# A rotary embedding whose inputs are freed by ScalarE and whose sums are made in SBUF, and two reorderings around it, in a two-block float32 kernel

## The reference, cut to what matters

```
proj = u @ in_w                                  # c_q (384), c_kv (256), k_r (64), z (2048)
q = (rms_norm(c_q, q_norm_w) @ uq_w)             # 16 heads of 128 + 64
kv = (rms_norm(c_kv, kv_norm_w) @ ukv_w)         # 16 heads of 128 (k) + 128 (v)
q_nope, q_rope = q[..., :128], rope(q[..., 128:], positions)
k_rope = rope(k_r, positions)                    # one for all heads
s = ([q_nope, q_rope] . [k_nope, k_rope]) * 192 ** -0.5, causal softmax, times v
o = o.reshape(...) * silu(z);  y = o @ out_w

rope(x): [x1 * cos - x2 * sin, x2 * cos + x1 * sin]
```

## Time and profile before

| | us |
|---|---|
| median of three runs | 941.56 |
| lowest, highest | 941.27, 942.48 |
| the profiled execution | 941.56 |
| its span in the trace | 939.7 |
| PE busy | 882.5 |
| mean granted TensorE clock | 0.973 of full |

### The profile page before, as it was taken

How to read it: one execution, slowest core, us unless ns; L and a number is a source line. 1 busy time by engine, 2 the same in 40 slices (tenths; PEclk the granted TensorE clock), 3 DMA queues, 4 the chain that set the end, 5 groups by cost and what they waited for, 6 DMA issues and landing times.

```text
span 939.7 us, 18247 instructions
## 1 busy us (share of the span) xinstructions
PE 882.5 (94%) x7019; PEld 847.8 (90%) x7019; DVE 555.1 (59%) x1569; ACT 481.9 (51%) x920; POOL 620.6 (66%) x274
## 2 busy tenths in 40 slices
PE   7999899999999899999999896978999999999995
PEld 7999899989998899999999885867899999999995
DVE  5987567762244434443369867676556666651165
ACT  6745555544445465555545265444464445554451
POOL 3899645547886355557777895333387888888980
PEclk9999999998999999999999898989999999999997
DMA  8666533333665234444645575131364666656631
GB/s 321 182 218 208 155 109 91 90 91 103 188 181 161 87 112 117 133 133 140 193 141 166 156 211 158 50 91 45 90 180 158 194 188 190 183 179 179 202 90 46
DMA packets 38534, 138.85 MB, mean 148 GB/s; under 512 B 4272, under 2 KB 4272, under 8 KB 38448
## 3 DMA queue, kind: packets, MB, share of 16 engines
q1 hardware_dynamic: 38448, 137.69, 48.7%
HBM read 136.63 MB, written 1.05 MB: 147 GB/s over the span
## 4 chain that ended last, share of the span: by engine, by line
PE 72%; DVE 11%; ACT 3%; issue 1%; POOL 1%; DVEq 0%; ACTq 0%
PE ps L541 19%; PE ps L542 19%; PE ps L543 19%; DVE ps L1526 2%; PE ps L566 1%; PE ps L737 1%; PE ps L739 1%; POOL wl L502 1%; PE ps L652 1%; PE ps L548 1%; PE ps L574 1%; DVE nnm L1680 1%; ACT wh L974 1%; PE ps L549 1%; PE ps L550 1%
## 5 line engine op out<-in xcount | busy, mean ns | idle before, releaser
L502 POOL TENSOR_TENSOR wl<-raw,wh 128x1024 fp32r<-128x1024 f32 x254 | 609.2, 2420 | 277.8 <-ACT wh L974 277.7
L541 PE MATMUL ps<-uh,wh 128*128 128x256 f32 x1248 | 354.8, 284 | 7.0 <-DVE ul L1461 3.0
L542 PE MATMUL ps<-ul,wh 128*128 128x256 f32 x1248 | 350.3, 281 | 0.0
L543 PE MATMUL ps<-uh,wl 128*128 128x256 f32 x1248 | 350.0, 280 | 0.0
L974 ACT ACTIVATE wh<-raw 128x1024 fp32r<-128x1024 f32 x256 | 263.0, 1054 | 121.5 <-PE ps L543 118.3
L541 PEld LDWEIGHTS ps<-uh,wh 128*128 128x128 f32 x1248 | 236.1, 189 | 12.1 <-issue 3.6
L542 PEld LDWEIGHTS ps<-ul,wh 128*128 128x128 f32 x1248 | 236.1, 189 | 0.0
L543 PEld LDWEIGHTS ps<-uh,wl 128*128 128x128 f32 x1248 | 235.6, 189 | 0.0
L1619 DVE TENSOR_TENSOR h<-ps,h 128x256 f32<-128x256 f32 x32 | 13.6, 424 | 118.0 <-PE ps L543 117.8
L542 PE MATMUL ps<-ffl,wh 128*128 128x256 f32 x176 | 49.3, 280 | 0.0
L541 PE MATMUL ps<-ffh,wh 128*128 128x256 f32 x176 | 49.1, 279 | 0.0
(11 more groups left out here) (361 smaller groups left out, 1794.8 us busy)
## 6 DMA issues: line engine op xcount, KB each, us to landing
raw<-slabs SPq DMA_DIRECT2D x256, 512.0 KB, 3.8
h<-x_fm SPq DMA_DIRECT2D x4, 256.0 KB, 5.4
out_fm<-outb SPq DMA_DIRECT2D x4, 256.0 KB, 2.2
cst<-shape_consts SPq DMA_DIRECT2D x1, 768.0 KB, 7.9
vec<-vectors SPq DMA_DIRECT2D x1, 303.5 KB, 4.0
pin<-p_fm SPq DMA_DIRECT2D x1, 256.0 KB, 5.7
```

The source lines that it names most:

```text
L502: nc.gpsimd.tensor_tensor(wl[:, s % PART_RING, :], raw[:, s % RAW_RING, :], wh[:, s % PART_RING, :].bitcast(f32), ALU.subtract).then_inc(s ...
L541: nc.tensor.matmul(res, w_h, a_h, start=first, stop=False)
L542: nc.tensor.matmul(res, w_h, a_l, start=False, stop=False)
L543: ins = nc.tensor.matmul(res, w_l, a_h, start=False, stop=last)
```

## The change

Five things are altered.

1. The `qr` projections have "act" as their consumer in the table: their bank is free when ACT has copied it to `rx`, no longer when DVE has read it. DVE's product with cos reads `rx` in SBUF.
2. The product with sin goes from `PS_TR` to a new SBUF tile `r1`, and signals `rope_swapped_read`. The add reads `r1` and `r2` in SBUF.
3. `rope_swap` waits for `rope_swapped_read` (the product) and not for `rope_out` (the add).
4. On ACT, `high_parts(n_q)` stands ahead of the copies of `v0`, no longer behind them. `feed("v0")`, which splits the slabs up to five ahead of `v0`'s, stands ahead of both, as it did.
5. On PE, `scores(0)` stands between the projections of head 0 and those of head 1.

```diff
-        add(f"qr{i}", "mla_uq_w", cols, "dve")
+        add(f"qr{i}", "mla_uq_w", cols, "act")
...
             def rope_swap(i):
 
-                if i:
-                    pe.wait_ge(sem("rope_copied"), i)
-                else:
-                    pe.wait_ge(sem("dve_evac"), freed[jobs["kr"].out][1])
+                who, count = freed[jobs[rope_job(i)].out]
+                pe.wait_ge(sem(f"{who}_evac"), count)
+                wait(pe, "rope_swapped_read", i)
+                if i == 0:
                     wait(pe, "xdt", 16)
-                wait(pe, "rope_out", i)
                 nc.tensor.matmul(PS_TR[:, 0:T], swap, rx[:, i % 2, :], start=True, stop=True)\
...
             head_proj(0)
+            scores(0)
             head_proj(1)
-            scores(0)
             scores(1)
...
             high_parts(n_kv)
+            feed("v0")
+            high_parts(n_q)
             for n in range(4):
                 for t in range(TB):
                     o = output(f"v{n}", t)
                     nc.scalar.activation(vn[:, t, n * 512:(n + 1) * 512], o[:, :], ACT.Copy).then_inc(sem("act_evac"), 1)
-                if n == 0:
-                    high_parts(n_q)
             for i in range(8):
                 o = output(f"qr{i}")
                 wait(act, "rope_out", i)
-                nc.scalar.activation(rx[:, (i + 1) % 2, :], o[:, 0:T], ACT.Copy).then_inc(sem("rope_copied"), 1)
+                nc.scalar.activation(rx[:, (i + 1) % 2, :], o[:, 0:T], ACT.Copy).then_inc(sem("act_evac"), 1)
...
+                who, count = freed[jobs[rope_job(i)].out]
+                dve.wait_ge(sem(f"{who}_evac"), count)
+                wait(dve, "rope_out", i)
+                tt(r2[:], rx[:, i % 2, :], cos, ALU.mult).then_inc(sem("rope_cos"), 1)
+                dve.wait_ge(sem("rope_swap"), i + 1)
+                tt(r1[:], PS_TR[:, 0:T], sin, ALU.mult).then_inc(sem("rope_swapped_read"), 1)
+                dve.wait_ge(sem("rope_swapped_read"), i + 1)
+                dve.wait_ge(sem("rope_cos"), i + 1)
                 if i == 0:
-                    taken("kr")
-                    tt(r2[:], rx[:, 0, :], cos, ALU.mult).then_inc(sem("rope_cos"), 1)
+                    tt(kr[0:64, 0, :], r1[0:64, :], r2[0:64, :], ALU.add)
+                    tt(kr[64:128, 1, :], r1[64:128, :], r2[64:128, :], ALU.add).then_inc(sem("rope_out"), 1)
                 else:
-                    o = output(f"qr{i - 1}")
-                    dve.wait_ge(sem("rope_copied"), i)
-                    wait(dve, "rope_out", i)
-                    tt(r2[:], o[:, 0:T], cos, ALU.mult).then_inc(sem("dve_evac"), 1)
-                turned = PS_TR[:, 0:T]
-                dve.wait_ge(sem("rope_swap"), i + 1)
-                tt(turned, turned, sin, ALU.mult).then_inc(sem("rope_sin"), 1)
...
-                    tt(qr[:, i - 1, :], turned, r2[:], ALU.add).then_inc(sem("rope_out"), 1)
+                    tt(qr[:, i - 1, :], r1[:], r2[:], ALU.add).then_inc(sem("rope_out"), 1)
```

More of the change, by code:

```diff
@@ L313, in build @@
         cqr, ckr = ar("cqr", [3, T]), ar("ckr", [2, T])
-        rx, r2 = ar("rx", [2, T]), ar("r2", [T])
+        rx, r1, r2 = ar("rx", [2, T]), ar("r1", [T]), ar("r2", [T])
         cursor[0] = mark
@@ L467, in gain, with rope_job @@
             return v(name, at + k)
+        def rope_job(i):
+            return f"qr{i - 1}" if i else "kr"
         block = ctx.enter_context(nc.Block())
@@ L748, in prob_transpose @@
                 if hd == 0:
-                    wait(pe, "rope_out", 9)
+                    wait(pe, "rope_swapped_read", 9)
                 for c in range(3):
@@ L1641, in rotate @@
                     nc.vector.memset(kr[0:64, 1, :], 0.0)
+                who, count = freed[jobs[rope_job(i)].out]
[6 more added lines that the diff above has]
+                dve.wait_ge(sem("rope_cos"), i + 1)
                 if i == 0:
-                    taken("kr")
-                    tt(r2[:], rx[:, 0, :], cos, ALU.mult).then_inc(sem("rope_cos"), 1)
-                else:
-                    o = output(f"qr{i - 1}")
-                    dve.wait_ge(sem("rope_copied"), i)
-                    wait(dve, "rope_out", i)
-                    tt(r2[:], o[:, 0:T], cos, ALU.mult).then_inc(sem("dve_evac"), 1)
-                turned = PS_TR[:, 0:T]
-                dve.wait_ge(sem("rope_swap"), i + 1)
-                tt(turned, turned, sin, ALU.mult).then_inc(sem("rope_sin"), 1)
[L1653 to L1659, removed]
-                    tt(qr[:, i - 1, :], turned, r2[:], ALU.add).then_inc(sem("rope_out"), 1)
+                    tt(kr[0:64, 0, :], r1[0:64, :], r2[0:64, :], ALU.add)
+                    tt(kr[64:128, 1, :], r1[64:128, :], r2[64:128, :], ALU.add).then_inc(sem("rope_out"), 1)
+                else:
+                    tt(qr[:, i - 1, :], r1[:], r2[:], ALU.add).then_inc(sem("rope_out"), 1)
             for n in range(2):
```

## The result

The changed kernel takes 949.07 us (median of four runs, 948.33 to 949.59), the kernel before 942.02 on the same chip; the ratio is 1.0067, with a 95% interval of 1.0044 to 1.0092. It was forecast at 943.4, between 941.3 and 944.5. The direction that the sum had was right and the size was not: it is slower by some 6 to 7 us, not by 1.9. The profiled execution took 947.84.

What follows compares the result with a forecast made beforehand. PE was taken to bound the kernel. From 941.56 us, +2.13 (high parts), -1.2 - 0.46 (rotations) and -0.1 (scores) made +0.37, and a clock fall +1.5, giving 943.4, range 941.3 to 944.5.

Steps and rivals of the forecast that it cites:

- the sum: All terms added to 941.56: +0.37 us without the clock and +1.5 for the clock, giving 943.4.
- What bounds the kernel, and that a loss before the head loop stays: PE bounds the kernel; a microsecond it gains or loses before the head loop is gained or lost at the end.
- Edit 4: `v1` at 289.39, net 2.13: Passage v0 to v1: v1 waits for v0's first copy, begins 2.57 later, 0.44 is regained, qr0 2.13 later.
- The clock: a fall, +1.5: PE's new 2.33 us pause before v1 brings 1.2 GHz for 3.3 to 3.4 us, costing 1.5; chance 0.55.
- the rival without a fall: Clock stays up behind the pause before v1; time 941.9, no difference; chance 0.27.
- the long spell: Low clock behind the pause before v1 holds 6.6 us, as at 212.40; time 945.0; chance 0.07.
- the spared fall: Clock stays up behind the 2.16 pause before 618.30, returning 1.6 us; 940.3 with no fall before v1; chance 0.06.
- Edits 1 to 3: -1.2 - 0.46: Rotations: with the add out of the swap loop, six steps save 1.2 us and the last pair 0.46.
- The rival "the rotations are not faster": ACT's copy with a slab split, or DVE, replaces the add as bound; 943.6 without fall, 945.1 with; chance 0.05.
- Edit 5: -0.1: scores(0) ahead of head_proj(1): pause moves from before the transposes to before the scores, 0.1 saved, bounds -0.2 and +0.3.

Runs made afterwards that it cites:

- e7: e2 plus six idle matmuls on PE behind the spread, filling some 2 us of the pause; 945.58 against 944.57 for the kernel before, ratio 1.0013.
- e2: Kernel before with only the high parts of q moved ahead of the copies of v0; 946.43 against 943.26, ratio 1.0028.
- e5: Whole change, but with r1 and a copy of cos in PSUM; 944.67 against 944.57 for the kernel before, ratio 1.0003.
- e6: Whole change, with POOL's instruction cut to 64 of 1024 columns for seven slabs (time probe only); 945.57 against 944.57 for the kernel before, ratio 1.0011.
- e4: Kernel before with only the rotation changes, r1 and a copy of cos in PSUM; 940.62 against 943.26, ratio 0.9983.
- e3: Kernel before with only scores(0) moved ahead of head_proj(1); 943.74 against 943.26, ratio 0.9997.
- e8: e4 with the last swap moved behind the projections of head 0; 940.91 against 944.57 for the kernel before, ratio 0.9975.
- e1: Kernel before with only the rotation changes, high parts and scores order undone; 945.23 against 943.26, ratio 1.0023.
- e9: e1 with r1 alone in PSUM, the cos product still reading SBUF twice; one run of 942.81 beside 943.70 for the kernel before.

## Why the prediction was wrong, step by step

- *What bounds the kernel, and that a loss before the head loop stays.* Right: S to T grew by 6.03 and the span by 6.3.
- *Edit 4: `v1` at 289.39, net 2.13.* Right to 0.03: it began at 289.42, and e7, where the clock stays up, has 2.13. The profile names no releaser for this pause ("issue"). That it waits for the first copy of `v0` rests on that copy's start at 288.74, 0.68 ahead of `v1` where 0.67 was forecast, and on e2, where edit 4 alone brings the pause.
- *The clock: a fall, +1.5.* Right in kind; e2 less e7 gives 1.26. In e5, where the clock was already low when `v1` began, the same stretch less e7's is 1.51, so the price varies with where the low spell lies. The fall came in all four profiled executions with the pause unfilled (the changed kernel, e2, e5, e6), so the rival without a fall did not occur. Neither did the long spell (the changed kernel's lasted from 290.35 to 293.76) nor the spared fall (the clock fell again behind the pause that ends at 624.59). The argument was weaker than it looked, though. It took two lone pauses just over 2 us as a sign of what such a pause does, and other profiles have pauses of 2 to 3 us without a fall (last section). In the kernel before a pause of 1.82, ending at 213.18, coincides with a fall too, so 2.16 was not the shortest, as the rival of the spared fall has it.
- *Edits 1 to 3: -1.2 - 0.46.* **This is the step that failed.** The mechanism was there: with the hold removed (e4, e5, e6) the rotations take 1.97 less, even 0.3 more than forecast, and the last pair of swaps is 1.21 apart, where I had 1.28. What failed is the sentence "DVE's product with cos and its add now read SBUF only. I take them at the add's 0.42 at most". That duration had been taken from an add with one input in PSUM, and the only rotation product with two SBUF inputs in the trace, 0.35 us, was a single case. In the changed kernel the instructions stood for POOL's, and the stretch was 16.67 and not 12.98: 3.69 of the miss. The same passage says that no one waits for these instructions until `scores(0)`. That is wrong too. ACT's next copy into `rx` waits for the add (`rope_out`), and the sine product, which frees `PS_TR` for the next swap, stands behind the cos product on DVE. One such copy of the changed kernel:

```profile
309.47 0.38 ACT L1138 ACTIVATE rx<-ps 128x256 f32<-128x256 f32 x1 [2.65 <-DVE qr L1657]
```

- *The rival "the rotations are not faster"* had the copies on ACT as its mechanism and a chance of 0.05. ACT's copies were late as well, but as a consequence: they wait for `rope_out`, DVE's add. e4 has the same copies and is fast. Its price, no gain at all, was also too small, since a hold can cost more than the add had.
- *Edit 5: -0.1.* 0.0 by itself (e3), and +0.61 in the changed kernel, since it put `scores(0)` directly behind the last rotation: the cover of 1.77 of `head_proj(1)`, which I had costed at nothing for this wait, was gone when the add ended 1.7 late.

The forecast sum was 1.87. The measured parts are 2.13 + 1.26 + 2.03 + 0.61 = 6.03; the other 0.3 of the span's 6.3 lies outside these stretches.

What could have been read beforehand stands in two places. The first is the trace of the kernel before, far from the rotations. It has the same instruction, an add of 128x256 with two SBUF inputs, eight times at line 1994 (durations in ns: shortest, median, longest), and others besides:

```profile
L1994 DVE TENSOR_TENSOR h<-h,pt x8: 424/859/2228, 904.0 to 927.7; 128x256 f32<-128x256 f32 x8
```
```profile
494.45 2.44 DVE L1762 TENSOR_TENSOR cpad<-cvt,csg 128x256 f32<-128x256 f32 x1
570.28 2.29 DVE L1857 TENSOR_TENSOR nrr<-nrr,gates 128x2 f32<-128x2 f32 x1
913.48 2.23 DVE L1994 TENSOR_TENSOR h<-h,pt 128x256 f32<-128x256 f32 x1
```

POOL's instructions around the last three run from 494.22 to 496.61, 570.16 to 572.56 and 913.01 to 915.42, and each of DVE's ends just behind. A median of twice the shortest duration is the sign to look for.

The second place: the Trainium skill, "SBUF — State Buffer", section "SBUF: two separate sides", says that DVE and GpSimd share one pair of SBUF ports, exclusively and for a whole instruction, and that a DVE instruction takes part in it when it has two SBUF inputs and GpSimd's reads SBUF. The trace agrees (DVE's ends 0.28 or 0.29 behind POOL's, five times). POOL is busy 66% of the span, and both of the moved operands turned a PSUM input into an SBUF one. By that rule each rotation would have had two instructions that can be held by POOL, and the gain would have had a rival of its own, on the other side.

## What to carry to other kernels

Before an operand of a VectorE instruction moves from PSUM to SBUF, look at its other input and at what GpSimd is doing: with two SBUF inputs beside a GpSimd instruction of 2.4 us, 0.42 became up to 2.5. A dependency that is shortened in the program can be longer in time; keep one input in PSUM (e4), and then fill what is left of the wait (e8). Before trusting one duration, compare the shortest and the median of an instruction in the whole trace. Where an instruction is moved ahead on an in-order engine, ask which bank the instructions behind it free, and count a possible fall of TensorE's clock behind the pause that arises.

## What the runs showed of the hardware

- A product or add of DVE with two SBUF inputs that starts while one of POOL's instructions runs stands until that one ends. Its own end comes the later behind it the larger it is: 0.02 us with 128x2 elements, 0.15 with 128x120 and 0.28 or 0.29 with 128x256 (kernel before, at 570.28, 505.28 and 494.45).
- One case is different. Where the product with cos of rotation 0 starts 0.19 to 0.20 behind POOL's recorded start (before, e1, e3, e9), it takes 0.35 all the same, and it is POOL's instruction that takes 2.80 or 2.81 instead of 2.40. A short distance to POOL's start isn't the rule for it: the one at 570.28 starts 0.12 behind and is held. What decides here is not shown. This case is why the kernel before looked harmless in the rotations.
- The other way round the cost goes by DVE's instruction. POOL's instructions that start while one of 128x256 with two SBUF inputs runs take 2.57 to 2.62 and not 2.38 to 2.40; the one that starts at 517.08 in the kernel before, while a DVE instruction of 128x2048 runs from 516.19 to 519.27, takes 4.41.
- TensorE's clock fell to 1.2 GHz behind the pause of 2.34 us before `v1` in each of the four profiles that leave it unfilled, and the pause of 1.70 before 671.32 left it alone. The Trainium skill, "TensorE: Matmul & The Clock Gate", section "Why this matters for your kernels", advises against pauses over about 3 us; here shorter ones were met by a fall. The length of one pause doesn't decide by itself: the clock stayed at 2.4 GHz behind 2.02 us in the changed kernel (ending at 316.06) and behind 2.19 and 2.99 us in e7, and it fell behind 1.32 us in e1 (ending at 904.74). What else decides is not shown. The two of e7, and the stretches behind them (granted clock third from last):

```profile
621.72 0.36 PE L541 MATMUL ps<-cnh,wh 128*128 128x256 f32 x1 [2.19 <-DVE cnl L1843]
...
656.48 0.52 PE L874 MATMUL ps<-cst,npn 128*128 128x128 f32 x3 [2.99 <-ACT cpT L1303]
...
621.70:625.20 3.50, 3.48 (x24) 2.95 (x25) 3.36 (x9) 3.47 (x10) 1.53 (x1) 1.00 0.29 117
656.50:659.90 3.40, 3.40 (x24) 2.75 (x25) 1.93 (x7) 2.26 (x4) 0.50 (x1) 1.00 0.00 0
```
